# The rotated half of queries and keys: from a matmul with a constant matrix to VectorE's stream shuffle

## The reference, cut to what matters

```python
def _rope_partial(x, cos, sin):                 # differential: 8 heads x 2 x 64 channels, ROT_DIM = 16
    x1 = x[..., :ROT_DIM // 2]
    x2 = x[..., ROT_DIM // 2:ROT_DIM]
    return jnp.concatenate([x1 * cos - x2 * sin, x2 * cos + x1 * sin, x[..., ROT_DIM:]], axis=-1)
...
dq = _rope_partial(_rms(dq.reshape(B, S, DIFF_HEADS, 2, DIFF_DK), diff_q_norm[l]), d_cos, d_sin)
dk = _rope_partial(_rms(dk.reshape(B, S, DIFF_HEADS, 2, DIFF_DK), diff_k_norm[l]), d_cos, d_sin)
...
def rope(x, pos):                               # sliding window: 16 query and 4 key heads x 64 channels
    half = x.shape[-1] // 2
    ...
    x1, x2 = x[..., :half], x[..., half:]
    return jnp.concatenate([x1 * cos - x2 * sin, x2 * cos + x1 * sin], -1)
```

## Time and profile before

| | us |
|---|---|
| median of 3 runs | 3236.79 |
| lowest, highest run | 3236.64, 3241.88 |
| the profiled execution's span | 3236.4 |
| TensorE busy in it | 3170.8 |
| VectorE, ScalarE, GpSimd busy | 1127.6, 1253.7, 1737.7 |

### The profile page before, as it was taken

How to read it: one execution, slowest core, us unless ns; L and a number is a source line. 1 busy time by engine, 2 the same in 40 slices (tenths; PEclk the granted TensorE clock), 3 DMA queues, 4 the chain that set the end, 5 groups by cost and what they waited for, 6 DMA issues and landing times.

```text
span 3236.4 us, 40309 instructions
## 1 busy us (share of the span) xinstructions
PE 3170.8 (98%) x15026; PEld 2599.2 (80%) x15026; DVE 1127.6 (35%) x2230; ACT 1253.7 (39%) x2260; POOL 1737.7 (54%) x1355
## 2 busy tenths in 40 slices
...
DMA packets 149840, 275.58 MB, mean 85 GB/s; under 512 B 16528, under 2 KB 17808, under 8 KB 149520
## 3 DMA queue, kind: packets, MB, share of 16 engines
...
## 4 chain that ended last, share of the span: by engine, by line
PE 92%; DVE 4%; ACT 1%; issue 1%; POOL 1%; DMA 0%; DVEq 0%; SPq 0%; ACTq 0%; POOLq 0%
PE PS L747 91%; PE PS L815 2%; DVE AR L1360 1%; DVE PS L1360 0%; DVE AR L1366 0%; ACT TMP L2134 0%; DVE TMP L1360 0%; POOL WL L2521 0%; DVE PS L2094 0%; POOL SM L2521 0%; DVE TMP L1366 0%; DVE ACC L1360 0%; DVE HL L1366 0%; DMA RAW<-in_wst 0%; ACT HH L2134 0%
## 5 line engine op out<-in xcount | busy, mean ns | idle before, releaser
L2521 POOL TENSOR_TENSOR WL<-RAW,WH 128x512 fp32r<-128x512 f32 x1002 | 1298.3, 1308 | 907.7 <-ACT WH L2134 906.8
L2134 ACT ACTIVATE WH<-RAW 128x512 fp32r<-128x512 f32 x1002 | 619.3, 627 | 1033.5 <-PE PS L747 973.6
L747 PE MATMUL PS<-HH,WH 128*128 128x512 f32 x2264 | 898.0, 397 | 6.7 <-DVE HL L1366 3.2
L747 PE MATMUL PS<-HL,WH 128*128 128x512 f32 x2264 | 886.1, 391 | 1.7 <-DVE HL L1366 1.7
L747 PE MATMUL PS<-HH,WL 128*128 128x512 f32 x2264 | 886.0, 391 | 0.0
L747 PE MATMUL PS<-AH,WH 128*128 128x512 f32 (+1 forms) x1504 | 584.6, 389 | 6.8 <-ACT AH L2134 4.4
L747 PE MATMUL PS<-AL,WH 128*128 128x512 f32 (+1 forms) x1504 | 581.9, 387 | 2.2 <-DVE AL L1360 1.1
L747 PE MATMUL PS<-AH,WL 128*128 128x512 f32 (+1 forms) x1504 | 581.9, 387 | 1.0 <-POOL WL L2521 1.0
L747 PEld LDWEIGHTS PS<-HH,WH 128*128 128x128 f32 x2264 | 427.7, 189 | 99.4 <-issue 11.2
L747 PEld LDWEIGHTS PS<-HL,WH 128*128 128x128 f32 x2264 | 427.7, 189 | 91.1 <-DVE HL L1366 4.4
L747 PEld LDWEIGHTS PS<-HH,WL 128*128 128x128 f32 x2264 | 427.2, 189 | 90.6
...
## 6 DMA issues: line engine op xcount, KB each, us to landing
...
```

What stands on the lines that cost most here:

```text
L747: return e.matmul(o, l, r, start=a, stop=z, skip_group_check=True)
L2134: return e.activation(o, a, f, **kw)
L2521: return e.tensor_tensor(o, a, b, op)
```

## The change

**Differential.** VectorE's stream shuffle permutes the partitions within each group of 32 and reads the projection straight from PSUM, as soon as ScalarE has squared it: `tmp(2+j)` gets the partners. A scalar-tensor-tensor then takes the projection out of PSUM with the norm's weight and the cosine table in one instruction, GpSimd multiplies the partners by the sine table (whose first half now has the minus sign), and a second scalar-tensor-tensor adds them with the partners' weights. Queries and keys no longer carry the input norm's factor: the head norm divides it out, and its epsilon is scaled by the matching variance (`eps_mix`) instead. TensorE's `d_rope` and VectorE's `d_gain` go. In `DIFF` `d_rope` and `d_add` stand behind each `d_q`; two entries of `LATE` go with them.

**Sliding window.** The weights' columns and the bias are laid out so that partners are 16 partitions apart, inside a group of 32. `sr(u)` is a shuffle of the tile behind the bias, and a product with the sine table in SBUF; the matmul goes. The order of the steps stays.

The two constant matrices leave `CST`. The diff, cut; `DIFF` is shown with two of its lines:

```diff
+DPAIR = [i + 8 if i < 8 else i - 8 if i < 16 else i for i in range(32)]
+SPAIR = [i ^ 16 for i in range(32)]
+
+
+def head_cols(c0):
+    return [(c0 + d, 1, 16) for d in (0, 32, 16, 48)]
+
+
+def in_pairs(a):
+    return np.concatenate([a[c:c + n] for c, _, n in head_cols(0)])
...
-            p += before + [("d_turn", h, 3), ("d_n", n)] + between + [("d_pv", h), ("d_rope", n, 0), ("d_rope", n, 1)] + behind
+            p += before + [("d_turn", h, 3), ("d_n", n)] + between + [("d_pv", h)] + behind
...
-        elif kind == "d_q" and i[1] == 0:
-            out += [s, ("d_gain", h)]
+        elif kind == "d_q":
+            out += [s, ("d_rope", *i), ("d_add", *i)]
...
-        elif kind == "d_rope":
-            out += [s, ("d_add", *i)]
...
 DIFF = [
...
-    ("d_sc", 0, 1), ("d_q", 1, 0), ("d_gain", 1), ("d_sm", 0, 0), ("d_sc", 0, 2), ("d_turn", 0, 0), ("d_sm", 0, 1), ("d_q", 1, 1), ("d_sc", 0, 3),
...
+    ("d_rope", 1, 0), ("d_add", 1, 0), ("d_sm", 0, 0), ("d_sc", 0, 2), ("d_turn", 0, 0), ("d_sm", 0, 1), ("d_q", 1, 1), ("d_rope", 1, 1),
...
-        ("vb", 2): 4, ("vb", 3): 4, ("x", ("nq", 0)): 4, ("x", ("nq", 1)): 4, ("x", ("nq", 2)): 4, ("x", ("nq", 3)): 4, ("d_rope", 2, 1): -4,
+        ("vb", 2): 4, ("vb", 3): 4, ("x", ("nq", 0)): 4, ("x", ("nq", 1)): 4, ("x", ("nq", 2)): 4, ("x", ("nq", 3)): 4,
         ("d_sm", 0, 0): -2, ("d_sm", 1, 0): -2, ("d_sm", 2, 0): -2, ("d_sm", 3, 0): -2, ("d_sm", 4, 0): -2, ("d_sm", 5, 0): -2,
...
-        ("d_rope", 2, 1): 2, ("d_sm", 0, 0): -2, ("d_sm", 1, 0): -2, ("d_sm", 2, 0): -2, ("d_sm", 3, 0): -2, ("d_sm", 4, 0): -2,
+        ("d_sm", 0, 0): -2, ("d_sm", 1, 0): -2, ("d_sm", 2, 0): -2, ("d_sm", 3, 0): -2, ("d_sm", 4, 0): -2,
...
                     turned(("d_normed", h), ("d_n", h), lambda t: quarter(tmp(3), t))
-                elif kind == "d_rope":
-                    h, j = i
-                    o = bank("d_roped", h, j)
-                    e.wait_ge(*at(("d_gain", "d_normed")[j], h))
-                    mm(o, CST[:, C_SWD:C_SWD + 128], ar(2 * (h % 2) + j), True, True).then_inc(*up("mm", "d_rope", h, j))
...
                         if q == 0 and r == 0:
                             e.wait_ge(*at("d_roped", h, 0))
-                            e.wait_ge(*at("d_roped", h, 1))
+                            e.wait_ge(*at("d_normed", h))
                         mm(o[:, 0:nk], ar(2 * (h % 2))[lo:lo + 64, 128 * q:128 * q + 128], ar(2 * (h % 2) + 1)[lo:lo + 64, 0:nk],
...
                     tok_row(opened[kind], k, "w_qkv_c_2", 0, 1280, 256, "H", k == 0, k == 7, ("sv",) if k == 7 else None)
-                elif kind == "sr":
-                    u = i[0]
-                    o = bank("s_sin", u)
-                    e.wait_ge(*at("s_bias", u))
-                    mm(o, CST[:, C_SWC:C_SWC + 128], ar(u), True, True).then_inc(*up("mm", "sr", u))
...
@@ -1374,8 +1372,13 @@
 
                 mult = NORM[n][1]
                 e.wait_ge(*at("mm", *(done or ("fac", n))))
-                ts(nwt(n, 0), held(n, 0), mult, EPS, MUL, ADD).then_inc(*up("var", n))
-                ts(held(n, 1), held(n, 0), mult, EPS, MUL, ADD).then_inc(*up("var_held", n))
+                if n[0] == "nd":
+                    eps = eps_mix.to_broadcast([128, 4, 4])
+                    stt(nwt(n, 0), held(n, 0), mult, eps, MUL, ADD).then_inc(*up("var", n))
+                    stt(held(n, 1), held(n, 0), mult, eps, MUL, ADD).then_inc(*up("var_held", n))
+                else:
+                    ts(nwt(n, 0), held(n, 0), mult, EPS, MUL, ADD).then_inc(*up("var", n))
+                    ts(held(n, 1), held(n, 0), mult, EPS, MUL, ADD).then_inc(*up("var_held", n))
 
...
                     be, bo = psum("r_even", h, j), psum("r_odd", h, j)
```

```diff
                         e.wait_ge(*(at("mm", "d_sc", h - 2, 3, 1) if h > 1 else at("mm", "r_sc", 3, 3)))
-                    tt(ar(2 * (h % 2) + j), psum("d_q", h, j), RB, MUL).then_inc(*up("d_q", h, j))
+                    if h == 0 and j == 0:
+                        e.wait_ge(*at("table", 0, 3))
+                    stt(ar(2 * (h % 2) + j), psum("d_q", h, j), vcol(("dq", "dk")[j]), tab(2), MUL, MUL).then_inc(*up("d_q", h, j))
                 elif kind == "d_v":
                     h = i[0]
                     e.wait_ge(*at("mm", "d_v", h))
                     e.wait_ge(*(at("mm", "fac", ("nt", h - 2)) if h > 1 else at("r_lo", 3, 1)))
                     tt(tmp(1), psum("d_v", h), RB, MUL).then_inc(*up("d_v", h))
                 elif kind == "d_f":
+                    if i[0] == 0:
+                        e.wait_ge(*at("eps_mix"))
                     variance(("nd", i[0]))
                 elif kind == "d_wide":
                     h = i[0]
                     e.wait_ge(*at("factor", ("nd", h)))
-                    e.wait_ge(*(at("d_cos", h - 1, 1) if h else at("r_lo", 3, 3)))
                     src = held(("nd", h), 1)[:, :, 2:4].unsqueeze(3).to_broadcast([128, 4, 2, 64])
                     e.tensor_copy(tmp(3).rearrange("p (a b c) -> p a b c", a=4, b=2), src).then_inc(*up("d_wide", h))
                     ts(eighth(h), held(("nd", h), 1)[:, :, 0:2], 0.125, None, MUL).then_inc(*up("d_eighth", h))
-                elif kind == "d_gain":
-                    q = ar(2 * (i[0] % 2))
-                    e.wait_ge(*at("d_square", i[0], 0))
-                    ts(q, q, vcol("dq"), None, MUL).then_inc(*up("d_gain", i[0]))
                 elif kind == "d_n":
                     h = i[0]
                     s = ar(2 * (h % 2) + 1)
                     e.wait_ge(*at("mm", "d_n", h))
-                    e.wait_ge(*at("d_square", h, 1))
-                    stt(s, s, vcol("dk"), psum("d_normed", h), MUL, MUL).then_inc(*up("d_normed", h))
-                elif kind == "d_rope":
-                    h, j = i
-                    r = psum("d_roped", h, j)
-                    e.wait_ge(*at("mm", "d_rope", h, j))
-                    if h == 0 and j == 0:
-                        e.wait_ge(*at("table", 0, 3))
-                    tt(r, r, tab(3), MUL).then_inc(*up("d_sin", h, j))
+                    e.wait_ge(*at("d_roped", h, 1))
+                    tt(s, s, psum("d_normed", h), MUL).then_inc(*up("d_normed", h))
                 elif kind == "d_add":
                     h, j = i
-                    q, r, s = tmp(2 + j), psum("d_roped", h, j), ar(2 * (h % 2) + j)
-                    e.wait_ge(*at("d_cos", h, j))
+                    s = ar(2 * (h % 2) + j)
+                    e.wait_ge(*at("d_q", h, j))
                     e.wait_ge(*at("d_sin", h, j))
-                    tt(s, q, r, ADD).then_inc(*up("d_roped", h, j))
+                    stt(s, tmp(2 + j), vcol(("dqp", "dkp")[j]), s, MUL, ADD).then_inc(*up("d_roped", h, j))
                 elif kind == "d_sc":
                     h, q = i
```

```diff
@@ -2066,8 +2065,10 @@
                 elif kind == "sr":
                     u = i[0]
                     q, r = tmp(3 + 2 * (u % 2)), tmp(4 + 2 * (u % 2))
-                    e.wait_ge(*at("mm", "sr", u))
-                    tt(r, psum("s_sin", u), tab(1), MUL).then_inc(*up("s_sin", u))
+                    e.wait_ge(*at("s_bias", u))
+                    e.stream_shuffle(r, ar(u), SPAIR).then_inc(*up("s_pair", u))
+                    e.wait_ge(*at("s_pair", u))
+                    tt(r, r, tab(1), MUL).then_inc(*up("s_sin", u))
                     e.wait_ge(*at("s_cos", u))
                     e.wait_ge(*at("s_sin", u))
                     tt(ar(u), q, r, ADD).then_inc(*up("s_roped", u))
@@ -2234,9 +2235,9 @@
                     act(g_tile(br, m), g_tile(br, m), ACT.Sigmoid, bias=vcol("bg", 8 * br + m)).then_inc(*up("sigmoid", br, m))
                 elif kind == "d_q":
                     h, j = i
-                    e.wait_ge(*at("d_q", h, j))
+                    e.wait_ge(*at("mm", "d_q", h, j))
                     e.wait_ge(*at("mm", "fac", ("nd", h - 1) if h else ("nr", 3)))
-                    act(tmp(4 + j), ar(2 * (h % 2) + j), ACT.Square).then_inc(*up("d_square", h, j))
+                    act(tmp(4 + j), psum("d_q", h, j), ACT.Square).then_inc(*up("d_square", h, j))
...
                 elif kind == "d_rope":
                     h, j = i
-                    e.wait_ge(*at(("d_gain", "d_normed")[j], h))
-                    if j == 0 and h:
-                        e.wait_ge(*at("d_roped", h - 1, 0))
+                    e.wait_ge(*at("d_pair", h, j))
                     if h == 0 and j == 0:
                         e.wait_ge(*at("table", 0, 3))
-                    tt(tmp(2 + j), ar(2 * (h % 2) + j), tab(2), MUL).then_inc(*up("d_cos", h, j))
+                    tt(tmp(2 + j), tmp(2 + j), tab(3), MUL).then_inc(*up("d_sin", h, j))
                 elif kind == "d_t2":
                     h = i[0]
                     e.wait_ge(*at("do_hi", h))
```

(8 more changed lines are left out.)

91 lines of the change are left out of this document (49 added, 42 removed).

## The result

| | before | after |
|---|---|---|
| median, us | 3236.95 (4 runs) | 3262.89 (4 runs) |
| lowest, highest | 3236.64, 3241.88 | 3261.99, 3264.64 |
| profiled span | 3236.4 | 3260.8 |

The ratio is 1.0075, 95% interval 1.0062 to 1.0088: the change makes the kernel 25.9 us slower. The forecast was 3244, range 3228 to 3253. The direction held; the size was missed by 19 us, and the time lies outside the range.

The account below looks back on a forecast made before the run. TensorE was taken to bound the kernel, VectorE also near full in the window stage. 3236.4 − 13.7 + 15.3 + 4.8 + 1 − 0.3 = 3243.5, with 0.4 for the median 3244 us; 8-in-10 range 3228 to 3253.

Parts of the forecast that it names:

- matmuls removed: Differential stage, TensorE: 16 rotation matmuls at 0.855 us go, −13.7 us if nothing takes their place.
- seven waits before the first transposes: Differential stage, heads 0 to 6: TensorE waits for the softmax quarter, now behind the next head's shuffle and scaling; +15.3 us.
- lower clock in the stage: Differential stage: TensorE falls to 1.2 GHz after long waits; +4.8 us (0 to 10).
- smaller terms: other waits: Differential stage: VectorE holds `d_add` behind GpSimd's product, so the value's eviction can come late; +1 us (0 to 4).
- sliding-window part: Window stage: TensorE loses 10 matmuls, some 9 us, but VectorE gains ten shuffles and leads; net −0.3 us (−3 to +3).
- three falls of eight matmuls: Differential stage: three waits each drop TensorE's clock, eight matmuls at 0.2 us more making 1.6 us each.
- the middle: Window stage, 2676 to 2755: VectorE's own path sets the length, 80.1 us with six shuffles more, +1.1.
- The head: Window stage's start: VectorE's wait for the first rotation shrinks, GpSimd's products become late; 1.1 to 1.7 gained, 1.4 taken.
- main case: Whole kernel: the summed terms hold, 3237 to 3252 us; chance 60%, about half of it under 3243.3.
- slow shuffle: Rival, both stages: a shuffle takes 1.2 us, waits and window stage grow, 3256 us (3252 to 3268); chance 10%.
- 10% and a third of 20% faster: Rivals: real gain, `d_turn(h,0)` hardly waits, 3214 to 3224 (10%); waits half as long, 3232 (20%).
- The shuffle, 0.61: VectorE's price for one 512-element shuffle, taken as the pitch of such an operation from PSUM; ends 0.4 and 1.2 us.

Follow-up runs that it names:

- both: Changed kernel with the first softmax quarter ahead of the shuffle and the sums behind the next scores' masks on VectorE; 3233.1 us, ratio 0.9978.
- diff_only: Changed kernel with the sliding-window part taken back to its matmuls; 3260.7 us, ratio 1.0065.
- rope_twice: Kernel before with each of the 16 differential products with the constant issued twice; 3252.8 us, ratio 1.0041.
- both_old_swa: Changed kernel with the quarter ahead of the shuffle, the sums late, and the sliding-window part as before the change; 3227.0 us, ratio 0.9963.
- both_pairs_first: both_old_swa with VectorE's shuffle and scaling before ScalarE's square; 3225.8 us, ratio 0.9963.
- swa_shuffle_twice: Kernel before with the change's sliding-window part alone, each of its 10 shuffles issued twice; 3250.3 us, ratio 1.0039.

## Why the prediction was right or wrong

The terms, as forecast and as the two profiled executions have them:

| term | forecast, us | measured, us |
|---|---|---|
| matmuls removed | −13.7 | −12.8 (by `both`) |
| seven waits before the first transposes | +15.3 | +16.8 |
| lower clock in the stage | +4.8 | +15.3 (8.7 in diff_only's execution) |
| smaller terms: other waits | +1 | +5.4 |
| sliding-window part | −0.3 | +2.6 |
| between the stages | 0 | −3.4 |

The measured ones add up to 23.9 of the 24.4 between the spans.

**Direction: right, and so is the first wait.** The wait that takes the place of the matmuls is the one that was named, at the instruction that was named. But it is one of two causes. Seven waits, forecast 15.3 us net of head 2's old one; measured 17.7 − 0.94 = 16.8. Heads 0, 2 and 6 are within 0.12 of the forecast. In heads 1, 3 and 4 it was 2.93 for 2.15, 3.77 for 3.2 and 2.92 for 2.3. One thing explains most of the three: the 128 x 128 product took 1.12 instead of 0.35, since GpSimd had begun its product with the sine table 0.3 us before it (in head 3 at 936.84), the one that the change gave it. Head 5 was 2.13 for 2.9: the square had no panel in front of it there.

**Matmuls removed, 13.7: right,** by rope_twice, and at most 2 us too much by `both` and both_old_swa.

**Clock, 4.8: the term that was most off.** I took three falls of eight matmuls, by the threshold of one row at 2.40 us and one at 1.88. The stage had eight stretches at the lower clock and fifty wide matmuls in them (+9.8), and the short transposes and scores in the same stretches slowed as well: 15.3 us in all. TensorE runs at 1.2 GHz there, and the length of the wait before isn't the measure: a wait of 1.25 us at 776.86 was followed by eight slow matmuls, the one of 2.13 at 802.75 by none. In diff_only the same wait of 1.24 was followed by none, nor were those of 2.94 and 2.92 in heads 2 and 4, which were in after. So a price worked out per wait could not be right but by luck; what the waits bring is a chance of a fall each. That the falls come with more idle time is what the traces show together: the stages of before, `both` and both_old_swa have none (8.3 to 10.0 us idle), those with 25 us or more have 25 to 60 slow matmuls. It isn't a rule for each: both_pairs_first, with 8.8 us, has 15, behind waits of 1.24 and 1.44 that other executions have without any.

**Smaller terms, +1 (0 to 4): the step that failed in kind.** "VectorE now holds `d_add` behind GpSimd's product" was written down and priced as a side effect. The waits beyond the seven grew by 5.4 us in after (22.2 − 16.8), and this was the small part: the sum's wait was a second full cause lying behind the first. With the quarter mended alone, 25.3 of 30.5 us of idle time remained (19.5 of the 25.0 in the stage's length). Head 0 shows it plainly. VectorE twice, then TensorE:

```profile
770.35 1.68 DVE L1364 SCALAR_TENSOR_TENSOR AR<-TMP,VC,AR 128x512 f32<-128x512 f32 x1 [2.67 <-POOL TMP L2522]
...
774.54 1.67 DVE L1364 SCALAR_TENSOR_TENSOR AR<-TMP,VC,AR 128x512 f32<-128x512 f32 x1 [1.21 <-POOL TMP L2522]
776.13 0.68 DVE L1358 TENSOR_TENSOR TMP<-PS,RBT 128x512 f32<-128x512 f32 x1
...
776.86 0.66 PE L822 MATMUL PS<-CST,TMP 128*128 128x128 f32 x4 [1.25 <-DVE TMP L1358]
```

Two waits for GpSimd (2.67, 1.21), two sums at 1.68 and 1.67 beside it, and the values' eviction comes at 776.13, for which TensorE waits 1.25.

**Sliding-window part, −0.3 (−3 to +3): right that TensorE's 9 us don't appear,** wrong by 2.9 on the size. Split at the first transposes (2676.05 before, 2700.78 after), the middle was forecast as +1.1 and is 0.5 shorter; that VectorE is its bound held (swa_shuffle_twice). The head was forecast to gain 1.4 and lost 3.1: the product had moved from PSUM into SBUF, and it and the sums stood behind GpSimd's instructions there. I priced the shuffle and not this move of an operand; the rows of before had sums between 0.69 and 1.29 us at that place, and I took them as one size.

**The range.** Its top, 3253, is that of the main case and leaves out most of the slow shuffle. What happened, more clock and more VectorE waits than counted, wasn't priced as a rival: the two terms were given ends (0 to 10, 0 to 4) and these ends weren't carried into the range. 3244 + 5 + 3 + 3 would have been 3255, and still short. The chances don't follow from their own parts either: 10% and a third of 20% faster, half of 60% and the rest of the 20% within, half of 60% and 10% slower are 0.17, 0.43 and 0.40, not 0.18, 0.36 and 0.46.

**The shuffle, 0.61: right.** None of the earlier trace rows shows that figure, since they give durations; the nearest in that trace are products from PSUM of this size that start 0.60 apart (395.98 to 397.79). The estimate from the Trainium skill (VectorE: DVE Perf Modes, the perf-mode tier table), 0.6 us for a shuffle of 512 elements, agrees with the 0.62 between starts.
